# Reordered weight splits, evictions and squares in a two-layer hybrid trunk kernel, with its constants loaded in three pieces

## The reference, cut to what matters

```python
def rms_norm(x, g):
    y = x * rsqrt(mean(x * x, axis=-1) + 1e-6)
    return y * g

h = h + 0.5 * rms_norm(swiglu(rms_norm(h, g[0]), w_gu, w_down), g[1])
h = h + rms_norm(mixer(rms_norm(h, g[2])), g[3])
h = h + 0.5 * rms_norm(swiglu(rms_norm(h, g[4]), w_gu, w_down), g[5])
```

## Time and profile before

| | |
|---|---|
| median of 3 runs | 2439.37 us |
| profiled execution | 2434.7 us, its span 2432.7 us |
| TensorE clock granted, mean | 0.938 |
| PE share of the chain that ended last | 82% |
| DVE, POOL, ACT shares of it | 10%, 3%, 3% |
| mean DMA rate | 75 GB/s |

### The profile page before, as it was taken

How to read it: one execution, slowest core, us unless ns; L and a number is a source line. 1 busy time by engine, 2 the same in 40 slices (tenths; PEclk the granted TensorE clock), 3 DMA queues, 4 the chain that set the end, 5 groups by cost and what they waited for, 6 DMA issues and landing times.

```text
span 2432.7 us, 51184 instructions
## 1 busy us (share of the span) xinstructions
PE 2253.0 (93%) x22812; PEld 1914.1 (79%) x22812; DVE 1114.4 (46%) x1471; ACT 791.9 (33%) x1347; POOL 579.3 (24%) x676
## 2 busy tenths in 40 slices
PE   6999998889689998979999999999998887999997
PEld 4888886678489974768888878888877656888886
DVE  4433326884655544554342364333274435533423
ACT  4333313751233321343333153333132333433320
POOL 2111104576132210341110141111062103311103
PEclk9999999889699996889999999999998669999999
DMA  4323311211000010223333113233113002233311
GB/s 150 116 93 118 120 59 54 97 63 36 1 3 4 4 37 18 105 91 105 105 110 117 53 61 127 93 122 118 56 61 104 0 0 83 92 105 105 122 70 35
DMA packets 28661, 183.37 MB, mean 75 GB/s; under 512 B 3184, under 2 KB 7856, under 8 KB 9504
## 3 DMA queue, kind: packets, MB, share of 16 engines
q1 hardware_dynamic: 27600, 178.79, 21.0%
q0 software_dynamic: 848, 1.37, 0.3%
HBM read 174.31 MB, written 4.30 MB: 73 GB/s over the span
## 4 chain that ended last, share of the span: by engine, by line
PE 82%; DVE 10%; POOL 3%; ACT 3%; issue 1%; DMA 0%; SPq 0%; POOLq 0%; DVEq 0%; ACTq 0%
PE psum L286 65%; PE psum L1499 6%; POOL h L346 2%; PE psum L2305 1%; PE psum L2306 1%; PE psum L1490 1%; PE psum L310 1%; DVE arena L383 1%; PE psum L1831 1%; PE psum L361 1%; PE psum L1523 1%; PE psum L2272 1%; DVE split L261 1%; ACT split L255 1%; PE psum L1833 1%
## 5 line engine op out<-in xcount | busy, mean ns | idle before, releaser
L286 PE MATMUL psum<-x,split 128*128 128x256 f16 (+2 forms) x5424 | 620.8, 276 | 8.7 <-POOL x L397 5.7
L286 PEld LDWEIGHTS psum<-x,split 128*128 128x128 f16 (+1 forms) x5424 | 532.8, 98 | 92.0 <-issue 9.3
L286 PE MATMUL psum<-x,split_more 128*128 128x256 f16 (+1 forms) x2688 | 314.1, 278 | 7.5 <-DVE split_more L261 5.2
L693 POOL TENSOR_TENSOR arena<-arena 128x256 f16<-128x256 f32 (+1 forms) x176 | 120.4, 684 | 785.7 <-ACT arena L543 785.7
L286 PEld LDWEIGHTS psum<-x,split_more 128*128 128x128 f16 x2688 | 266.1, 99 | 50.4 <-DVE split_more L261 5.5
L286 PE MATMUL psum<-arena,split 128*128 128x256 f16 (+2 forms) x2448 | 278.2, 276 | 4.0 <-ACT arena L1205 4.0
L286 PE MATMUL psum<-x,arena 128*128 128x256 f16 (+1 forms) x2400 | 275.8, 276 | 3.6 <-POOL x L928 3.4
L286 PEld LDWEIGHTS psum<-arena,split 128*128 128x128 f16 (+1 forms) x2448 | 240.7, 98 | 39.6 <-ACT arena L1205 4.7
L261 DVE SCALAR_TENSOR_TENSOR split<-stage,split 128x2048 f16<-128x2048 f32 (+2 forms) x77 | 192.2, 2496 | 170.2 <-ACT split L255 170.2
L286 PEld LDWEIGHTS psum<-x,arena 128*128 128x128 f16 x2400 | 234.7, 98 | 39.3 <-POOL x L928 5.6
L620 DVE SCALAR_TENSOR_TENSOR arena<-psum,arena 128x256 f32<-128x256 f32 (+1 forms) x176 | 75.5, 429 | 327.9 <-ACT arena L537 323.3
(11 more groups left out here) (220 smaller groups left out, 2830.3 us busy)
## 6 DMA issues: line engine op xcount, KB each, us to landing
stage<-in_w_gu SPq DMA_DIRECT2D x88, 1024.0 KB, 4.9
stage<-in_w_down SPq DMA_DIRECT2D x32, 1408.0 KB, 6.1
stage<-in_w_rkv SPq DMA_DIRECT2D x12, 1024.0 KB, 4.9
stage<-in_w_out SPq DMA_DIRECT2D x4, 1024.0 KB, 4.8
stage<-in_w_q SPq DMA_DIRECT2D x4, 1024.0 KB, 4.8
stage<-in_w_o SPq DMA_DIRECT2D x4, 1024.0 KB, 5.5
h_spill<-h SPq DMA_DIRECT2D x1, 2112.0 KB, 8.5
h<-h_spill SPq DMA_DIRECT2D x1, 2112.0 KB, 9.6
```

The lines of the kernel that those rows point to most:

```text
L286: last = pe.matmul(o, wt(wp, k), xs(xp, k), start=(k == 0 and wp == 0 and xp == 0), stop=(k == tiles - 1 and wp == 1))
L693: e.tensor_tensor(hid[s][:, 1, m, 0:n], hid32[:, no % 2, 0:n], hid[s][:, 0, m, 0:n], ALU.subtract).then_inc(hid_lo, 1)
```

## The change

In hand-overs 1, 3 and 4 ACT squares five of the eight h tiles, then output tile 5 of half 1, makes the high split of job 1, and squares the other three h tiles; the split of job 2 goes behind the squares of the last output tile instead of ahead of them. DVE follows with the last two evictions side by side. In hand-overs 2 and 5 the high split of job 0 goes between the third and the fourth h tile, the split of job 1 ahead of `pre_root` and `pre_inverse`, the split of job 2 behind the last squares and evictions, and PE's `pre_total` of half 0 comes twelve matmuls later. In the opening h is squared ahead of the first split, the split of job 3 goes ahead of the x of half 1, the ones are loaded by themselves ahead of the first weights, and the vectors and the other constants behind them; PE waits for the ones alone, and DVE for the rest. `early` moves to hand-over 1.

```diff
@@ -160,6 +160,7 @@
         done = sem("step_products")
         freed = sem("banks_freed")
         s_in = sem("vectors_landed")
+        s_ones = sem("ones_landed")
         s_x = [sem(f"x_landed_{q}") for q in range(4)]
         s_out = sem("output_stored")
         eps_set = sem("eps_set")
@@ -543,8 +544,8 @@
                     e.activation(hid[s][:, 0, m, 0:n], hid32[:, no % 2, 0:n], ACT.Copy).then_inc(hid_hi, 1)
 
                 if opening:
+                    square_h(e, T, 0)
                     split_hi(e, ups[0])
-                    square_h(e, T, 0)
                     pre_root(e, T, 0)
                     T.how.high(e, T, 0)
                     split_hi(e, ups[1])
@@ -553,8 +554,8 @@
                     pre_root(e, T, 1)
                     gate(0, 0)
                     high(0, 0)
+                    split_hi(e, ups[3])
                     T.how.high(e, T, 1)
-                    split_hi(e, ups[3])
                     gate(1, 0)
                     high(1, 0)
                 else:
@@ -602,14 +603,15 @@
                         squares(m, 1)
                     post_root(e, T_out, 1)
                     return
-                square_h(e, T_out, 0)
+                square_h(e, T_out, 0, 0, 5)
                 squares(5, 1)
                 split_hi(e, T_out.jobs[1])
+                square_h(e, T_out, 0, 5, KT)
                 pre_root(e, T_out, 0)
                 T_out.how.high(e, T_out, 0)
                 squares(6, 1)
+                squares(7, 1)
                 split_hi(e, T_out.jobs[2])
-                squares(7, 1)
 
             def dve(e):
                 def gated(m, s):
@@ -633,8 +635,8 @@
                     split_lo(e, ups[2])
                     pre_inverse(e, T, 1)
                     gated(0, 0)
+                    split_lo(e, ups[3])
                     T.how.scale(e, T, 1)
-                    split_lo(e, ups[3])
                     gated(1, 0)
                 else:
                     post_inverse(e, T, 1)
@@ -683,8 +685,8 @@
                 pre_inverse(e, T_out, 0)
                 T_out.how.scale(e, T_out, 0)
                 evict(6, 1)
+                evict(7, 1)
                 split_lo(e, T_out.jobs[2])
-                evict(7, 1)
 
             def pool(e):
                 def rest(m, s):
@@ -769,7 +771,7 @@
                     out(j, 0)
                 out(0, 1, ((1, 0), post_total))
                 out(1, 1)
-                out(2, 1, ((0, 4), pre_total))
+                out(2, 1, ((1, 0), pre_total))
                 out(3, 1)
 
             def act(e):
@@ -782,16 +784,17 @@
                 for j in range(4):
                     squares(j, 0)
                 post_root(e, T_out, 0)
-                square_h(e, T_out, 0)
+                square_h(e, T_out, 0, 0, 3)
+                split_hi(e, T_out.jobs[0])
+                square_h(e, T_out, 0, 3, KT)
                 squares(0, 1)
-                split_hi(e, T_out.jobs[0])
+                split_hi(e, T_out.jobs[1])
                 squares(1, 1)
                 pre_root(e, T_out, 0)
                 T_out.how.high(e, T_out, 0)
-                split_hi(e, T_out.jobs[1])
                 squares(2, 1)
+                squares(3, 1)
                 split_hi(e, T_out.jobs[2])
-                squares(3, 1)
 
             def dve(e):
                 def evict(j, s):
@@ -806,12 +809,12 @@
                 evict(0, 1)
                 split_lo(e, T_out.jobs[0])
                 evict(1, 1)
+                split_lo(e, T_out.jobs[1])
                 pre_inverse(e, T_out, 0)
                 T_out.how.scale(e, T_out, 0)
-                split_lo(e, T_out.jobs[1])
                 evict(2, 1)
+                evict(3, 1)
                 split_lo(e, T_out.jobs[2])
-                evict(3, 1)
 
             def pool(e):
                 def sums(j, s):
@@ -888,6 +891,7 @@
                 def scale(dve, T, s):
                     a, n = T.spans[s]
                     if s == 0:
+                        early(dve)
                         dve.memset(hn[:, :, 0:PAD], 0.0).then_inc(padded.sem, padded.step("hn"))
                     for k in range(KT + 2):
                         if k < KT:
@@ -2444,9 +2448,12 @@
             a, n = HALF[0]
             for q in range(2):
                 sp.dma_start(h[:, 4 * q:4 * q + 4, 0:n], xT[:, 4 * q:4 * q + 4, 0:n]).then_inc(s_x[q], 16)
-            sp.dma_start(cst[:, :], consts).then_inc(s_in, 16)
+            o1 = CST["ones"][0]
+            sp.dma_start(cst[:, o1:o1 + P], consts[:, o1:o1 + P]).then_inc(s_ones, 16)
+            first_ffn.first_load(sp)
             sp.dma_start(vec[:, :], vecs).then_inc(s_in, 16)
-            first_ffn.first_load(sp)
+            sp.dma_start(cst[:, 0:o1], consts[:, 0:o1]).then_inc(s_in, 16)
+            sp.dma_start(cst[:, o1 + P:NCST], consts[:, o1 + P:NCST]).then_inc(s_in, 16)
             for q in range(2):
                 sp.dma_start(h[:, 4 * q:4 * q + 4, n:L], xT[:, 4 * q:4 * q + 4, n:L]).then_inc(s_x[2 + q], 16)
             first_ffn.sync(sp)
@@ -2463,7 +2470,7 @@
 
         @block.scalar
         def _(act):
-            act.wait_ge(eps_set, 3)
+            act.wait_ge(eps_set, 2)
             warm(act, ACT.Sqrt)
             first_ffn.scalar(act)
             mixer_0.scalar(act)
@@ -2476,12 +2483,11 @@
         def _(dve):
             dve.memset(eps[:, 0:1], RMS_EPS).then_inc(eps_set, 1)
             dve.memset(eps[:, 1:2], GN_EPS).then_inc(eps_set, 1)
-            dve.wait_ge(s_in, 32)
+            dve.wait_ge(s_in, 48)
 
             gn = v("gain", 0, 2 * 6 * KT).rearrange("p (l w k) -> p l w k", l=2, w=6)[:, :, 1::4, :]
             dve.tensor_scalar(gn, gn, 0.5, None, ALU.mult).then_inc(eps_set, 1)
             dve.wait_ge(eps_set, 3)
-            mixer_0.early(dve)
             first_ffn.vector(dve)
             mixer_0.vector(dve)
             second_ffn.vector(dve)
@@ -2501,8 +2507,9 @@
 
         @block.tensor
         def _(pe):
-            pe.wait_ge(s_in, 32)
+            pe.wait_ge(s_ones, 16)
             first_ffn.tensor(pe)
+            pe.wait_ge(s_in, 48)
             mixer_0.tensor(pe)
             second_ffn.tensor(pe)
             third_ffn.tensor(pe)
```

## The result

The kernel after took 2395.72 us (median of 4 runs, 2393.34 to 2398.09), the kernel before, on the same chip, 2439.39 (2438.69 to 2440.73). The ratio is 0.9821, its 95% interval 0.9808 to 0.9833. The profiled execution of after took 2393.34 us with a span of 2391.4, against 2434.7 and 2432.7 before. The medians differ by 43.7 us, the profiled pair by 41.4; 43.7 was forecast for either. That the median came within 0.1 us is therefore partly luck, and what follows goes by stretches of the traces.

A forecast was written before the change was run, and what follows sets the result against it. PE, busy 93% of the span, was bounding; only its standstills, chiefly 42.4 us waiting for POOL's sums, could be won. Terms 11.1 + 4.1 + 7.4 + 5.9 + 5.2 + 10.0 = 43.7 us gave a 2395.7 us median, range 2388 to 2412.

The forecast's parts named there:

- The forecast of about 10 us: All hand-overs: PE's wait on POOL's sums falls from 42.4 to about 10 us.
- Opening, 11.1 forecast: Opening: earlier pre_inverse gives 6.2 us, no wait on the fourth weight tile gives 4.9; together 11.1 us.
- Hand-over 3, 5.9: Hand-over 3: post_total 4.2 us sooner and full clock behind it 1.7 us more; 5.9 us, bounds 3.3 and 6.5.
- (a): Hand-overs: DVE's moved low split makes PE wait in pre_total of half 1; 35 us won in all, 2404; chance 0.10.
- Hand-over 4, 5.2: Hand-over 4: same as hand-over 3 with a shorter stretch at low clock; 5.2 us, bounds 3.3 and 6.5.
- Hand-over 2, 7.4: Hand-over 2: only sums stand between x and the last eviction; 7.4 us with DVE's split first, bounds 5.2 to 10.
- the race for the last add: Hand-overs 2 and 5: whether POOL's last add_h or DVE's low split starts first; split first gives 2.2 us less.
- Hand-over 5, 10.0: Hand-over 5: splits moved as in hand-over 2, but POOL's add starts 0.1 us ahead; 10.0 us, bounds 7.4 to 11.
- hand-over 1, 4.1: Hand-over 1: post_total at 406.2 in place of 410.29, new 2.6 us PE standstill costing nothing; 4.1 us, bounds 2 and 5.
- (b): Contention with POOL wherever a low split runs beside it: 2.2 us in hand-over 5, about 0.7 in three others; 2400; chance 0.12.
- (c): Hand-overs: POOL's x rest, not the squares, holds post_total, so only the opening is won; 2428 us; chance 0.05.
- (d): Slower: splits ahead of DVE's norm work delay post_inverse of half 1, 2.5 us per hand-over; 2445.7 us; chance 0.03.

The follow-up runs named there:

- The parts alone: Two runs on the kernel before: loads and squares of the opening alone, 2432.41 us; split of job 3 ahead of x of half 1 alone, 2434.80 us.
- The whole squares: Kernel after with the eight h squares together ahead of job 1's split in hand-overs 1, 3 and 4, job 2's split still late; 2397.19 us.
- the part alone: Kernel before with the new order in hand-overs 2 and 5 alone; 2420.45 us, ratio 0.9925.
- the repeat of after: Kernel after run once more, unchanged, on another chip; 2396.05 us, ratio 0.9825 to the kernel before.
- the kernel with both mends: Kernel after with tile 5's eviction ahead of job 0's low split in hand-over 1, and that split behind POOL's last add_h in 2 and 5; 2393.79 us.

## Why the prediction was right, and where it was off

**The bound** was read rightly: PE's waits on POOL's sums, caused by splits ahead of the last squares. They fell by 28.3 us, the squares being earlier by what stood in front of them. The forecast of about 10 us for what is left came from the hand-overs, and there it fits (2.66, 4.17, 0.39, 0.51 and 3.63: 11.4); the other 2.7 us of the 14.1 are three further waits, which that sum left out.

**Opening, 11.1 forecast, 11.17 measured.** The steps hold: weights split from 8.92 us (9.1 forecast; at its own 0.35 MB per us the 544 KB were 1.55 us and not 1.4, and 1.61 was measured), DVE free at about 13.2 (13.35), first product at 17.07 (17.2), no wait on the fourth weights. The parts alone gave 5.9 and 5.6 (6.2 and 4.9).

**Hand-over 3, 5.9 against 5.80.** Both halves of the term came: the wait shrank to 0.39 us (0.45 forecast), and the matmuls behind it run at 0.121 us. The inverse of half 1 stands at 1396.97, 27.04 us behind the mark, where it stood 30.34 us behind it: 3.3 us, as forecast. PE's wait in `pre_total` of half 1, the sign of rival (a), is at most 0.47 us here and 0.65 in hand-over 4. The whole squares showed that the split of the squares, worked out at 1.0 us, is worth 0.64 of it.

**Hand-over 4, 5.2 against 4.8** up to the point where PE resumes; attention then gave back 0.6, which is less than that stretch varies between executions of one kernel.

**Hand-over 2, 7.4 against 7.17.** In the race for the last add the split was first: 9.34 us for eight adds (9.2 forecast), and keeping it back gave 7.19. The sum left out a second meeting: the low split of job 1 lies beside POOL's two sums, which take 3.40 us in place of 1.59; what this costs no run isolates. **Hand-over 5, 10.0 against 10.55:** here POOL was first, 6.82 us (6.8 forecast). Up to the last inverse it gained 9.96; the rest lies in the feed-forward behind, which varies (11.18 for the whole stretch in the part alone, 9.6 and 9.7 in two other profiles). The Trainium skill (GPSIMD Engine Reference, section Specifications) has VectorE and GpSimd contend for their shared SBUF interface when a VectorE instruction reads two SBUF inputs. The trace agrees in both hand-overs. The row doesn't say which engine pays; the prediction took it to be POOL ("hand-over 5 would pay as well"). At the last add of 5 the trace shows DVE paying, 2.72 us for a split of 2.29, and POOL only afterwards, with a copy of 1.59 us beside the same split that took 0.40 in before.

**The step that was off: hand-over 1, 4.1 against 2.4.** The place and the wait were right, 2.81 us in `pre_total` (2.6 forecast). What was mis-sized is "`pre_inverse` gains 0.5, ... clock unchanged". It was to come 16.0 us after the mark and `post_total` 30.6; in after's profile they came at 17.03 and 31.80, where before has 16.52 and 34.67. Of the missing 1.7 us, 1.0 lies ahead of `pre_inverse`, 0.2 between it and `post_total`, 0.3 in the 30 matmuls behind (4.86 us, in before 4.59), and 0.2 in the mixer. `early` has no part in the first: it stands behind `pre_inverse` and costs 0.3 us there, from the inverse to the memset (2.29 us, in before 1.99).

The six matmuls behind the standstill took 2.42 us, 0.40 each, where sixteen in a row take 4.17, 0.26 each. The windows view of that stretch (length, busy time of PE, PEld, DVE, ACT, POOL, then granted clock, DMA share, GB/s) gives a clock of 0.67, a stretch between the 1.2 and the 2.4 GHz level. But this belongs to the execution. The same order with the same standstill in the repeat of after, its six matmuls and its window, shows the full clock; in the run with `pre_total` at its old place the clock is lower still. First after, then the repeat, then that run:

```profile
378.40:380.80 2.40, 2.31 (x7) 1.59 (x8) 2.04 (x1) 0.68 (x3) 0.00 (x0) 0.67 0.60 249
...
378.23 1.64 PE L362 MATMUL psum<-arena,cst 128*128 128x272 f32 x6 [2.80 <-ACT arena L356]
378.14:380.54 2.40, 2.31 (x14) 1.91 (x15) 2.15 (x2) 1.16 (x4) 0.00 (x0) 1.00 0.59 242
...
378.56 2.98 PE L362 MATMUL psum<-arena,cst 128*128 128x272 f32 x6 [2.80 <-ACT arena L356]
378.47:380.87 2.40, 2.31 (x5) 1.75 (x6) 2.04 (x1) 0.67 (x3) 0.00 (x0) 0.55 0.57 236
```

In six profiles with this standstill the clock right behind it was 1.00 three times and 0.74, 0.67 and 0.55 in the others; what decides between them was not found. At 1.00 `pre_inverse` comes at 16.24 and `post_total` at 31.00, 0.2 and 0.4 us behind the forecast. So 0.8 of the missing 1.7 is the clock of one execution. (The 84 matmuls behind `pre_total` took 10.27 us in place of 9.33 in after, their first 3.2 us at a clock of 0.72, but this costs nothing: PE waits 2.66 us for POOL's sums behind them, as it does in the repeat.) On average the stretch is 633.0 us in the five profiles with after's order and 636.2 in the four with the old one, a gain of 3.1; it is the forecast 4.1 that was too much, by about 1 us.

Where the prediction said of the 2.6 us that they cost nothing, it looked at PE alone. PE stands still because three squares of h stand behind the late split of job 1, and `pre_inverse` and all that follows wait for these squares as well. The eviction put ahead of the low split showed it: no standstill, `pre_inverse` at 13.78, 2.5 us ahead of the 16.24, and the same 2.66 us of wait at `post_total`.

**Rivals.** (a) fell, with its margin known: 0.65 us of wait in hand-over 4. (b) fell in hand-over 5 and held in 2, where the forecast had it; of its 0.7 us in the three others nothing shows in 3, where 5.80 came for 5.9. (c) fell: the squares held `post_total`, and the wait shrank by 28.3 us with them. What is left in 2 and 5 does come from POOL, whose sums now follow its x rest without a gap (four sums, 3.3 us each time). (d) fell: `post_total` moved in every hand-over.

## What to carry to other kernels

Where an engine waits late in a chain, look at what stands in the written-out order of the engines ahead of the last small instructions: here 2 us splits stood in front of 0.4 us evictions and squares, and moving them behind paid nearly all of what the rows said. Put a short instruction that others wait for ahead of a long one that nobody needs yet, and where instructions of two engines slow each other, see which comes first: a delay of 0.8 us on DVE saved POOL 2.15. An engine's standstill may cost nothing by itself and still show that something it waits for is late for others too. Compare edits by stretches of the trace between fixed marks, since a median over a kernel of this length can hide 3 to 5 us of real gain; and where the clock falls in a stretch, look at a second execution before you name it as the cause.

## What was not expected

**The attention stretch varies by itself.** From the last inverse of hand-over 4 to the first of hand-over 5 the same instructions took 221.3 to 231.4 us in 14 profiles, in the order of the granted clock. Windows of that stretch in after, and in the kernel with both mends:

```profile
1776.86:1999.79 222.93, 198.19 (x1233) 147.90 (x1231) 92.60 (x157) 61.72 (x187) 49.73 (x92) 0.79 0.15 44
```

```profile
1772.23:2003.60 231.37, 210.27 (x1233) 154.16 (x1231) 92.61 (x158) 61.25 (x187) 49.73 (x92) 0.74 0.14 42
```

PE's busy time grows by 12.08 us, that of DVE, ACT and POOL stays within 0.5. The kernel after alone gave 222.93 at 0.79 and 226.72 in its repeat. What decides the clock that this stretch is granted was not found.

**Who starts first wins a long instruction.** The same pair, POOL's last add and DVE's low split, went the one way in hand-over 2 and the other in 5, and came out the same way in the repeat of after (9.33 and 6.81 us for the adds, 9.34 and 6.82 before). The later one got through when the other was done: that cost POOL 2.15 us (9.34 less 7.19), against a split of 2.27, and DVE 0.43 (2.72 less 2.29).
